# The order of the gram products in block 1's recurrence

## The reference, cut to what matters

```
# wkv7_scan, per head:  S_t = S_{t-1} (diag(w_t) + a_t b_t^T) + v_t k_t^T ;  y_t = S_t r_t
for d, reverse in enumerate((False, True)):
    s_c, yc = wkv7_scan(r_c, dc, kc, vr_c, ac, bc, s0, reverse, with_ctx_out)   # 256 context tokens
    _, yl  = wkv7_scan(r_l, dl, kl, vr_l, al, bl, s_c, reverse, True)           # 512 latent tokens
    y_l = yl if y_l is None else y_l + yl
```

## Time and profile before

| | |
|---|---|
| runs | 4084.21, 4084.24, 4094.86 us; median 4084.24 |
| the profiled execution | 4094.25 us, its span 4092.3 us |
| mean granted TensorE clock | 0.916 of full speed |
| PE, PEld | busy 87%, 64% of the span |
| DVE, ACT, POOL | busy 39%, 27%, 3% of the span |
| the six steps of the recurrence | from about 430 to 960 us of the span |

### The profile page before, as it was taken

One profiled execution on the slowest core, in us unless ns is written; L12 is line 12 of the kernel. 1 busy time (PEld: TensorE's weight loads), 2 busy tenths in 40 slices (PEclk: granted clock), 3 DMA queues, 4 the chain that ended last, 5 costly groups with the idle time before them and its releaser, 6 DMA issues. The chain is left out here.

```text
span 4092.3 us, 53439 instructions
## 1 busy us (share of the span) xinstructions
PE 3552.0 (87%) x23544; PEld 2639.4 (64%) x23544; DVE 1584.9 (39%) x2436; ACT 1111.3 (27%) x1687; POOL 118.2 (3%) x149
## 2 busy tenths in 40 slices
PE   6988778885798788599998779999999998689999
PEld 5844667774443233488877547887788786467877
DVE  3455554443611111533332634333433434534333
ACT  2234332221100000222232453222322323453222
POOL 0000010000000000100000000000000000000000
PEclk8999777776799999799999989999999999899999
DMA  6120000002189998332221003322232221012321
GB/s 219 62 103 21 2 2 3 3 2 102 62 320 409 409 409 351 112 100 85 103 83 67 1 8 105 103 83 103 83 103 85 85 78 67 1 59 78 100 99 41
DMA packets 198899, 441.28 MB, mean 108 GB/s; under 512 B 6299, under 2 KB 97933, under 8 KB 198669
## 3 DMA queue, kind: packets, MB, share of 16 engines
q1 hardware_dynamic: 198668, 437.86, 29.3%
HBM read 435.75 MB, written 2.10 MB: 107 GB/s over the span
## 5 line engine op out<-in xcount | busy, mean ns | idle before, releaser
L335 PE MATMUL banks<-mix_r,ring_r 128*128 128x512 f32 x1776 | 702.0, 395 | 0.0
L335 PE MATMUL banks<-mix_r,ffn_r 128*128 128x512 f32 x1664 | 666.1, 400 | 14.9 <-ACT mix_r L2150 7.8
L335 PE MATMUL banks<-h_r,ffn_r 128*128 128x512 f32 x1664 | 652.0, 392 | 0.0
L297 DVE TENSOR_TENSOR ring_r<-ring,ffn_r 128x2048 fp32r<-128x2048 f32 (+1 forms) x169 | 359.6, 2128 | 228.9 <-ACT ffn_r L294 226.0
L294 ACT ACTIVATE ffn_r<-ring 128x2048 fp32r<-128x2048 f32 (+1 forms) x169 | 301.3, 1783 | 478.9 <-PE banks L335 472.6
L335 PEld LDWEIGHTS banks<-mix_r,ring_r 128*128 128x128 f32 x1776 | 336.0, 189 | 83.3
L335 PEld LDWEIGHTS banks<-mix_r,ffn_r 128*128 128x128 f32 x1664 | 315.5, 190 | 83.9 <-issue 16.9
L335 PEld LDWEIGHTS banks<-h_r,ffn_r 128*128 128x128 f32 x1664 | 315.5, 190 | 73.5
L2327 PE MATMUL banks<-ring_r,ffn_r 128*128 128x512 f32 x704 | 279.2, 397 | 0.0
L1878 PE MATMUL banks<-ring,arena 128*64 128x512 f32 x1056 | 241.6, 612 | 37.6 <-DMA ring<-in_exp_w_down 26.2
L2326 PE MATMUL banks<-ffn_r 128*128 128x512 f32 x640 | 252.6, 395 | 4.7 <-DVE arena L2279 4.7
(11 more groups left out here) (393 smaller groups left out, 5299.5 us busy)
## 6 DMA issues: line engine op xcount, KB each, us to landing
ring<-in_exp_w_down SPq DMA_DIRECT2D x30, 2048.0 KB, 18.3
ring<-in_w_ffn_gate SPq DMA_DIRECT2D x44, 1024.0 KB, 5.4
ring<-in_w_ffn_up SPq DMA_DIRECT2D x44, 1024.0 KB, 8.0
ring<-in_w_ffn_down SPq DMA_DIRECT2D x20, 2048.0 KB, 7.7
ring<-in_exp_w_gate SPq DMA_DIRECT2D x18, 2048.0 KB, 18.2
ring<-in_exp_w_up SPq DMA_DIRECT2D x18, 2048.0 KB, 19.1
ring<-in_w_in SPq DMA_DIRECT2D x17, 2048.0 KB, 8.1
arena<-in_exp_w_gate SPq DMA_DIRECT2D x14, 2048.0 KB, 19.1
```

What stands on the lines that cost most here:

```text
L297: l.did(V.tensor_tensor(lo, x_, hi, ALU.subtract).then_inc(l.sem, 1), name, "lo", v)
L335: ins = TE.matmul(m[1](bank), m[2], m[3], start=m[4], stop=m[5])
```

## The change

All gram products are issued ahead of level 1, on TensorE and on VectorE. The levels and joins have none between them, and the table `of_gram` is gone. No instruction is added or removed: per step, six gram products (24 calls) and twelve VectorE reads are moved. The lists of ACT, POOL and SP don't change.

```diff
@@ core_pe
-                        gram(0)
-                        gram(1)
+                        for q in range(CELLS):
+                            gram(q)
                         for i in LEVELS:
                             level_p(i, 0)
                             level_p(i, 1)
-                            for q in of_gram[i]:
-                                gram(q)
                             level_x(i, 0)
                             level_x(i, 1)
                         pair_p(0)
                         pair_p(1)
-                        for q in of_gram[5]:
-                            gram(q)
                         pair_x(0)
                         pair_x(1)
-                        for q in of_gram[6]:
-                            gram(q)
                         whole_p(0)
                         whole_p(1)
@@ core_dve
                         gm(0, 0)
                         begin(1)
                         gm(0, 1)
-                        gm(1, 0)
-                        gm(1, 1)
+                        for q in range(1, CELLS):
+                            gm(q, 0)
+                            gm(q, 1)
                         for i in LEVELS:
                             add(i, 0)
-                            for q in of_gram[i]:
-                                gm(q, 0)
                             add(i, 1)
-                            for q in of_gram[i]:
-                                gm(q, 1)
                         pairs(0)
-                        for q in of_gram[5]:
-                            gm(q, 0)
                         pairs(1)
-                        for q in of_gram[5]:
-                            gm(q, 1)
-                        for q in of_gram[6]:
-                            gm(q, 0)
-                            gm(q, 1)
                         wholes(0)
                         wholes(1)
```

More of the change, by code:

```diff
@@ L1200, in step @@
                     lower, upper = (lambda d: banks[:, 4 + d, :]), (lambda d: banks[:, 6 + d, :])
-                    of_gram = {1: (2,), 2: (3,), 3: (4,), 4: (5,), 5: (6,), 6: (7,)}
                     def core_pe(l):
```

## The result

The changed kernel takes 4125.33 us (median of 4 runs, 4123.91 to 4131.52) against 4084.6 of the kernel before (4 runs): 1.0097 times, 95% interval 1.0078 to 1.0115. It is slower by 40.7 us; the forecast was 29 us. Taken again later with another set of runs of the kernel before (14, median 4082.39) it was 4117.24 us, 1.0091 times, 1.0077 to 1.0105, so 34.9 us. The profiled execution of the changed kernel took 4131.52 us.

What follows compares the result with a forecast made beforehand. PE was taken to wait for instruction pages in the levels. Delay +11.2, levels -2.5 and joins -3.8 gave +4.9 us a step, +29.4 on the 4084.2 median: about 4113 us, own range 4099 to 4129, whole range 4096 to 4142.

Steps and rivals of the forecast that it cites:

- What bounds the levels: In the levels PE waits for 256-instruction pages, about 3.65 us each; a gram product costs its 17 instructions, not 2.08 us.
- The start of level 1: Between gram(1) and the first P1 product: six gram products delay level 1 by 11.2 us a step.
- one slow stretch: Ahead of level 1, in some steps: 3.4 us at 2.01 instead of 1.32 us a cell cost 1.2 us.
- half-clock rival: Gram products ahead of level 1 stay at half clock: 14.8 us delay, +8.5 a step, 4135 us; chance 0.19.
- The levels: Levels without their four gram products: -2.5 us a step, with -1 and -4 as ends.
- the instructions of four gram products: In the levels: four gram products of 17 instructions each go, saving 1.0 us a step.
- POOL's wait: In level 1 the second P1 product no longer waits 1.68 us for POOL, in four of six steps: 1.1 us.
- The joins: Joins behind the levels, without gram(6), gram(7) and a DVE read: -3.8 us a step.
- all three parts: In the joins: second pair product 0.6 us earlier, gram(6) gone ahead of `pair_x` -2.0, gram(7) gone ahead of `whole_p` -1.15.
- The sum: Whole recurrence: 11.2 - 2.5 - 3.8 = +4.9 us a step, +29.4 for six.
- About nothing: Rival over all stretches: no slow stretch (10.4), levels -4, joins -4.2; +2.2 a step, near 4097 us; chance 0.10.
- The faster rival: Gram products, not pages, hold the levels: levels 15.5 instead of 30.7 us, -7.6 a step, 4039 us; chance 0.05.

## Why the prediction was right, point by point

**What bounds the levels.** Right, and shown three times: half the instructions halve the levels, a quarter more lengthens them by a fifth to a quarter, and leaving out four gram products of 2 us gives 2.5 us and not 8. What was too low is the price of a gram product there, 0.6 us measured where the 17 instructions alone give 0.25. In the run with more instructions 128 matmuls run in 1.35 us, and the next come 3.46 us after the first. The Trainium skill (Runtime: NRT & Kernel Launch, instruction fetch mechanics) calls the fetch hidden; by these rows it isn't for such small matmuls, and the measurement decides.

**The start of level 1: forecast +11.2, measured +11.5 and +11.9.** gram(2) started 9.61 us after the first own product, to the hundredth what the rows of before gave (523.05 - 513.44). At full clock the cells came 1.30 us apart (forecast 1.32). The term that was sized too low is the clock: I allowed 1.2 us for one slow stretch of 3.4 us, and only as part of a mean. In step 0 it held for 6 us on gram(2) to gram(4). In three of six steps (five of six windows of the second profile are 18.6 us or longer) this cost about 2 us, and only step 2, whose slow stretch lay ahead of gram(2), reached the full-clock figure of 17.3. The mean at full clock was also a little too high in my sum: from step 1's 6.63 us to the mean of 7.06 it is 0.4 us less, so 10.2 and not 10.4. The half-clock rival (14.8) did not come about in any step; the longest delay was 12.4.

**The levels: forecast -2.5, measured -2.1 and -3.0.** The sum is right, its split is not shown. I had -1.0 for the instructions of four gram products, -1.1 for POOL's wait, and the last -0.4 had no term of its own. The run without gram products still has POOL's wait (8.0 us in six steps) and gives -2.5 already; the run with two cells ahead has four gram products in the levels and no such wait and gives -1.4. The two don't add up to the -2.1 to -3.0 of both together. Part of the scatter may come from the page loads, whose requests in the levels of step 0 lie about 3.7 us apart in one profile of the changed kernel and 3.5 in the other; the two profiles of the kernel before differ by 0.3 us a step here.

**The joins: forecast -3.8, measured -3.8.** Right, in all three parts. They show in the timeline of step 1:

```profile
571.75 1.06 PE L1248 MATMUL banks<-arena 32*32 32x32 f32 x32 [1.56 <-DVE arena L1372]
...
574.08 0.90 PE L1248 MATMUL banks<-arena 32*32 32x32 f32 x26 [1.27 <-DVE arena L1372]
...
576.93 0.38 ACT L1345 ACTIVATE arena<-banks 32x256 f32<-32x256 f32 x1 [1.37 <-DVE arena L1392]
577.45 3.28 PE L1272 MATMUL banks<-arena 64*64 64x64 f32 x32 [0.76 <-DVE arena L1392]
```

The second pair product comes 2.33 us after the first where it was 2.93; `whole_p` is held by DVE's and ACT's copies, with 0.76 us of waiting, and starts 5.7 us after the first pair product instead of 9.6.

**The sum.** Forecast +29.4. The parts give +34 and +30.5, and from the first own product to the last product of the recurrence the two profiles of before took 521.6 and 524.5 us, those of the changed kernel 557.3 and 551.4, +31 in the mean. The distance between +29.4 and the +31 of the recurrence is small, partly because the clock's extra cost and the levels' gain offset each other in the second profile. The rest of the 35 to 41 us that the medians show is not in the recurrence, and the forecast had no term for it. The code ahead of it is the same in all these kernels, yet the first own product started between 427.3 and 437.6 us in thirteen profiles, at 437.6 in the first profile of the changed one. The sets of the kernel before had medians between 4082.4 and 4092.9. I didn't find what moves these, and left it open.

**The rivals.** "About nothing" failed at the levels, which gave 2 to 3 us and not 4, at the joins, which gave 3.8 and not 4.2, and at the clock. The faster rival was the one worth testing, and its own figure for a level's pace was about right (3.1 to 3.4 us, at full clock and with half the calls); what it got wrong is that this pace applies only once the instructions are fewer.

## What to carry to other kernels

Where PE runs many small matmuls, count its instructions between two gaps that nothing releases: if the count is the same each time, PE is waiting for instructions, and work with few instructions and much time (here 17 and 2 us) costs little there (0.6 us) and more where nothing covers it (1.9 each in the joins, about 1.9 each ahead of level 1). Before work is moved out of such a stretch, ask what covers it in its new place. Before it is moved in, look at what else its page holds: two gram products in one page took longer than a page load at half clock.

## What the runs showed of the hardware

In the levels the time follows the number of PE's instructions, not the columns that they stream: with 1024 fewer level instructions a step and the same columns the changed kernel lost 82 to 88 us, more than the whole reordering is worth either way. The ends of the gaps of the levels of step 0 lay 3.3 to 3.8 us apart in the changed kernel, five of six at a granted clock of 0.50; in the kernel before a page took 3.60 us at 0.98. The level products themselves are quicker: 128 matmuls with their weight loads ran in 1.35 us.
